# A two-layer hybrid decoder trunk in float32: tables loaded in pieces, adaptation sums and small DVE jobs moved, attention transposes and the key's rotary sum reordered

## What is computed

```python
for l in range(DEPTH):
    mod = c_act @ ada_w[l] + ada_b[l]                       # 6 * 1024 numbers from one vector c
    h = modulate(rmsnorm(x, mix_pre_g[l]), sh_m, sc_m)
    t = h @ w_in                                            # 1024 x 6816
    y_lru = rglru_branch(...) @ lru_wo                      # conv, gates, softplus(-lambda), linear scan
    y_ret = retention_branch(...) @ ret_wo                  # rotary q and k, decayed scores, group norm
    y_mla = mla_branch(...) @ mla_wo                        # low-rank q and kv, 8 heads, causal softmax
    merged = gates[0] * y_lru + gates[1] * y_ret + gates[2] * y_mla
    x = x + g_m * rmsnorm(merged @ w_out, mix_post_g[l])
    x = x + g_f * rmsnorm(conv_glu(h2, w_up, conv, w_down), ffn_post_g[l])
```

## Time and profile before

| | us |
|---|---|
| median of 3 runs | 958.68 (957.09 to 959.09) |
| the profiled execution, own time | 959.5 |
| its span in the trace | 957.7 |
| PE busy | 931.6 (97%) |
| DVE busy | 731.3 (76%) |
| ACT busy | 522.7 (55%) |
| DMA | 206.36 MB, mean 215 GB/s |

### The profile page before, as it was taken

One profiled execution on the slowest core, in us unless ns is written; L12 is line 12 of the kernel. 1 busy time (PEld: TensorE's weight loads), 2 busy tenths in 40 slices (PEclk: granted clock), 3 DMA queues, 4 the chain that ended last, 5 costly groups with the idle time before them and its releaser, 6 DMA issues.

```text
span 957.7 us, 17447 instructions
## 1 busy us (share of the span) xinstructions
PE 931.6 (97%) x6840; PEld 863.5 (90%) x6840; DVE 731.3 (76%) x988; ACT 522.7 (55%) x693; POOL 43.7 (5%) x85
## 2 busy tenths in 40 slices
PE   6999999999999999999999999999999999999997
PEld 6889899889987999999979999989999799999996
DVE  4969968877787878887786877887768776676666
ACT  4445756445557655454673475743446675554553
POOL 0000000100000000000000000000000000000000
PEclk9999999999999999999999999999999999999999
DMA  9995757775583676766645775767666455655451
GB/s 351 327 287 194 230 200 262 239 240 200 186 295 113 231 254 245 256 241 199 203 170 169 252 240 189 248 210 236 207 230 233 163 176 179 216 175 179 146 202 44
DMA packets 134427, 206.36 MB, mean 215 GB/s; under 512 B 6497, under 2 KB 104801, under 8 KB 134241
## 3 DMA queue, kind: packets, MB, share of 16 engines
q1 hardware_dynamic: 122704, 162.08, 51.5%
q0 software_dynamic: 11520, 41.95, 12.0%
q10 hardware_dynamic: 144, 1.51, 0.5%
HBM read 204.47 MB, written 1.05 MB: 215 GB/s over the span
## 4 chain that ended last, share of the span: by engine, by line
PE 80%; DVE 11%; DMA 3%; ACT 2%; issue 2%; SPq 1%; DVEq 0%; ACTq 0%; POOLq 0%
PE banks L1705 73%; DVE w_lo L1097 3%; DVE adw L1090 2%; DMA h<-in_ada_rows 1%; DMA raw<-in_w_in 1%; DMA adw<-in_ada_rows 1%; SPq L463 1%; PE banks L1995 1%; PE banks L1985 1%; PE banks L1988 1%; ACT h_hi L656 1%; PE banks L1816 1%; DVE EF L1607 1%; PE banks L1862 0%; PE banks L2004 0%
## 5 line engine op out<-in xcount | busy, mean ns | idle before, releaser
L1705 PE MATMUL banks<-h_lo,w_hi 128*128 128x256 f32 x1504 | 426.0, 283 | 5.9 <-DVE h_lo L1158 2.2
L1705 PE MATMUL banks<-h_hi,w_lo 128*128 128x256 f32 x1504 | 420.7, 280 | 0.0
L1705 PE MATMUL banks<-h_hi,w_hi 128*128 128x256 f32 x1504 | 420.4, 280 | 0.0
L1705 PEld LDWEIGHTS banks<-h_lo,w_hi 128*128 128x128 f32 x1504 | 283.3, 188 | 10.9 <-issue 4.9
L1705 PEld LDWEIGHTS banks<-h_hi,w_lo 128*128 128x128 f32 x1504 | 283.5, 188 | 2.3 <-issue 1.4
L1705 PEld LDWEIGHTS banks<-h_hi,w_hi 128*128 128x128 f32 x1504 | 283.4, 188 | 0.0
L1097 DVE TENSOR_TENSOR w_lo<-raw,w_hi 128x2048 fp32r<-128x2048 f32 x96 | 219.4, 2289 | 47.0 <-ACT w_hi L598 46.5
L598 ACT ACTIVATE w_hi<-raw 128x2048 fp32r<-128x2048 f32 x96 | 182.7, 1912 | 103.6 <-PE banks L1705 82.0
L1607 DVE SCALAR_TENSOR_TENSOR EF<-banks,par,EF 128x254 f32<-128x254 f32 (+1 forms) x176 | 76.8, 478 | 57.6 <-ACT EF L949 51.8
L1631 DVE TENSOR_TENSOR w_lo<-raw,w_hi 128x2048 fp32r<-128x2048 f32 x42 | 96.0, 2286 | 21.1 <-ACT w_hi L968 21.1
L968 ACT ACTIVATE w_hi<-raw 128x2048 fp32r<-128x2048 f32 x42 | 80.4, 1913 | 36.7 <-PE banks L1705 36.7
(11 more groups left out here) (275 smaller groups left out, 1210.8 us busy)
## 6 DMA issues: line engine op xcount, KB each, us to landing
raw<-in_w_in SPq DMA_DIRECT2D x52, 1024.0 KB, 5.8
raw<-in_ffn_w_up SPq DMA_DIRECT2D x44, 1024.0 KB, 5.1
adw<-in_ada_rows POOLq DMA_DIRECT2D x80, 512.0 KB, 4.9
raw<-in_ffn_w_down SPq DMA_DIRECT2D x22, 1024.0 KB, 4.9
raw<-in_w_out SPq DMA_DIRECT2D x8, 1024.0 KB, 7.3
raw<-in_ret_wo SPq DMA_DIRECT2D x4, 1024.0 KB, 6.7
raw<-in_lru_wo SPq DMA_DIRECT2D x4, 1024.0 KB, 6.9
raw<-in_mla_wo SPq DMA_DIRECT2D x4, 1024.0 KB, 7.1
```

What stands on the lines that cost most here:

```text
L1705: ins = MM(ps, lhs, rhs, start=first and n == 0, stop=last and n == 2)
```

## The change

The table comes in six pieces, issued by SP behind blocks 4 to 9: the rotation matrices first, then the decays two heads at a time, then the mask. PE's first rotation waits for the first piece only, and DVE waits for the rest ahead of the key's rotary sum of layer 0. The LRU gate weights are loaded by POOL, those of layer 0 when block 2 has its high part, those of layer 1 behind tile 25. The first two tiles wait for block 7 instead of 3. The adaptation sums of blocks 7 to 12 are gone; `merge_sums` has one more in m = 4 and 6 and two more in m = 8 and 9. The second `angles` and the stages of `softplus` stand earlier in DVE's and ACT's lists. The key's rotary sum stands ahead of the first two `ret_scores`. Both `head_scales` stand behind both value products. For even m below 8, the transposes stand behind the branch product, and `mla_av` stands in the middle of the next gate product; ACT's copy stands behind the split. The loop of POOL is the same loop in two parts.

```diff
--- before.py
+++ after.py
@@ -288,6 +288,8 @@
 
         col = {**COL, "-8sp": P + 120, "8sp": P + 124}
 
+        TABLES = [(NFIRST, c0), *((c0 + 2 * i * T, c0 + 2 * (i + 1) * T) for i in range(HEADS // 2)), (c0 + HEADS * T, NCONST)]
+
         def PC(l, name, i=0, n=1):
             return par[:, l, col[name] + i:col[name] + i + n]
 
@@ -300,7 +302,7 @@
         ADA0 = 2 * DK
 
         c_in, cst_in, pos_in, x_in, vec_in = (sem(n) for n in ("c_in", "cst_in", "pos_in", "x_in", "vec_in"))
-        tables_in = sem("tables_in")
+        rotations_in, tables_in = sem("rotations_in"), sem("tables_in")
         ada_in = [sem(f"ada_in{i}") for i in range(ADA0 // 2 + 1)]
         cbc_ps, cbc_ev = sem("cbc_ps"), sem("cbc_ev")
         ada0_used, ada0_red, wbd_zero = sem("ada0_used"), sem("ada0_red"), sem("wbd_zero")
@@ -482,13 +484,9 @@
                         sp.dma_start(pos_i, A["positions"][0, :].partition_broadcast(P)).then_inc(pos_in, 16)
                         sp.dma_start(par[:, 0, 0:2 * P], A["vectors"][:, 0, 0:2 * P]).then_inc(vec_in, 16)
                         sp.dma_start(par[:, 1, :], A["vectors"][:, 1, :]).then_inc(vec_in, 16)
-                    if j == 4:
-
-                        sp.wait_ge(wbd_zero, 1)
-                        for m, name in enumerate(("lru_wa", "lru_wx")):
-                            for b in range(2):
-                                blockw = A[name][bass.ds(l, 1)].rearrange("a (i b) h k -> (a b) h i k", b=2)[b]
-                                sp.dma_start(wbd[64 * b:64 * b + 64, m, :, 64 * b:64 * b + 64], blockw).then_inc(wbd_in.s, 16)
+                    if l == 0 and 4 <= j < 4 + len(TABLES):
+                        a, b = TABLES[j - 4]
+                        sp.dma_start(cst[:, a:b], consts[:, a:b]).then_inc(rotations_in if j == 4 else tables_in, 16)
 
                 def up(l, c0, n):
                     return A["ffn_w_up"][bass.ds(l, 1)].rearrange("a (k p) n -> p (a k) n", p=P)[:, :, bass.ds(c0, n)]
@@ -536,21 +534,38 @@
 
             ada_v = A["ada_rows"].rearrange("l (t p) d -> p (l t) d", p=P)
             TILES = 2 * NT * L - ADA0
-            assert TILES % 2 == 0
+            assert TILES % 2 == 0 and L == 2
 
             def load(n, slot):
                 pool.dma_start(adw[:, slot, :], ada_v[:, bass.ds(n + ADA0, 1), :].rearrange("p a d -> p (a d)")).then_inc(adw_in[slot], 16)
 
             pool.wait_ge(ada0_red, ADA0 - len(ON_PE))
             pool.wait_ge(ada0_used, len(ON_PE))
-            pool.wait_ge(hi_ready.s, hi_ready.at(0, 4))
+            def recurrence_weights(l):
+
+                for m, name in enumerate(("lru_wa", "lru_wx")):
+                    for b in range(2):
+                        blockw = A[name][l].rearrange("(i b) h k -> b h i k", b=2)[b]
+                        pool.dma_start(wbd[64 * b:64 * b + 64, m, :, 64 * b:64 * b + 64], blockw).then_inc(wbd_in.s, 16)
+
+            def next_tiles(first, last):
+
+                with pool.Fori(first // 2, last // 2) as it:
+                    for slot in range(2):
+                        pool.wait_ge(ada_red.s, it * 2 + (1 + slot))
+                        pool.sem_inc(tick, 1)
+                        load(it * 2 + (2 + slot), slot)
+
+            pool.wait_ge(wbd_zero, 1)
+            pool.wait_ge(hi_ready.s, hi_ready.at(0, 3))
+            recurrence_weights(0)
+            pool.wait_ge(hi_ready.s, hi_ready.at(0, 8))
             load(0, 0)
             load(1, 1)
-            with pool.Fori(0, TILES // 2 - 1) as it:
-                for slot in range(2):
-                    pool.wait_ge(ada_red.s, it * 2 + (1 + slot))
-                    pool.sem_inc(tick, 1)
-                    load(it * 2 + (2 + slot), slot)
+            next_tiles(0, NT)
+            pool.wait_ge(lr_ev.s, lr_ev.at(0, 2))
+            recurrence_weights(1)
+            next_tiles(NT, TILES - 2)
 
 
 
@@ -739,12 +754,15 @@
 
                 split_block(l, 3)
                 if l == 0:
-                    act.dma_start(cst[:, NFIRST:NCONST], consts[:, NFIRST:NCONST]).then_inc(tables_in, 16)
                     act.wait_ge(vec_in, 48)
                 for j in range(4, 9):
                     split_block(l, j)
-                    if l == 0 and j in (4, 8):
-                        sines((0, 2)[j // 8])
+                    if l == 0 and j in (4, 6):
+                        sines(j - 4 if j == 4 else 2)
+                    if l == 0 and j == 7:
+                        softplus_exp()
+                    if l == 0 and j == 8:
+                        softplus_log()
 
                 for i in range(2):
                     product_done(act, l, J[("lx", i)])
@@ -753,8 +771,6 @@
                                scale=PC(l, "lru_conv_w", 12 + t), bias=PC(l, "lru_conv_b", t))
                     a.then_inc(lx_c0.s, 1)
                     split_block(l, 9 + i)
-                    if l == 0:
-                        (softplus_exp, softplus_log)[i]()
 
 
                 def lru_gates(i):
@@ -912,9 +928,11 @@
                     if m == 9:
                         attended_high(1)
                     gate(m)
-                    if m % 2 == 0 and 2 <= m <= HEADS:
+                    if m == HEADS:
                         transposed(m // 2 - 1)
                     split_block(l, j + RING + m % 2)
+                    if m in (2, 4, 6):
+                        transposed(m // 2 - 1)
                     if m == 6:
                         attended_high(0)
                     if m % 2 == 1 and m < HEADS:
@@ -1283,8 +1301,8 @@
                 V.scalar_tensor_tensor(flat2(CD, c).rearrange("p (h n) -> p h n", n=64), vsum[:, c, :].unsqueeze(2).to_broadcast([P, 8, 64]),
                                        -1.0 / 64, heads, ALU.mult, ALU.add).then_inc(v_ev.s, 1)
 
-            mixer_sums = {j: n for n, j in enumerate(range(7, 21))}
-            merge_sums = (2, 1, 2, 1, 2, 1, 2, 1, 1, 1, 2, 2)
+            mixer_sums = {j: n for n, j in enumerate(range(13, 21))}
+            merge_sums = (2, 1, 2, 1, 3, 1, 3, 1, 3, 3, 2, 2)
             assert len(mixer_sums) + sum(merge_sums) == NT + DK
 
             def mixer_split(l, j):
@@ -1322,16 +1340,18 @@
                 dve.wait_ge(trig_ready, 2)
                 rope_parts(0)
                 mixer_split(l, 5)
+                if l == 0:
+                    angles(sinm, cosm, inv_mla)
+                    softplus(0)
                 rope_parts(1)
                 mixer_split(l, 6)
                 mixer_split(l, 7)
+                if l == 0:
+                    softplus(1)
                 rope_parts(2)
                 rope_sum(0)
                 rope_parts(3)
                 rope_sum(1)
-                if l == 0:
-                    angles(sinm, cosm, inv_mla)
-                    softplus(0)
                 mixer_split(l, 8)
 
                 def ret_scores(h):
@@ -1374,12 +1394,10 @@
                 rope_sum(2)
                 mixer_split(l, 9)
                 if l == 0:
-                    softplus(1)
+                    softplus(2)
                 rope_sum(3)
                 lru_taps(1)
                 mixer_split(l, 10)
-                if l == 0:
-                    softplus(2)
                 latent_low(0)
                 latent_low(1)
                 mixer_split(l, 11)
@@ -1410,9 +1428,11 @@
 
                 dve.wait_ge(lr_ev.s, lr_ev.at(l, 2))
                 V.tensor_tensor(h32[:, 0:4, :], h32[:, 0:4, :], EF[:, 0:4, :], ALU.mult).then_inc(l_ix.s, 1)
+                if l == 0:
+                    dve.wait_ge(tables_in, 16 * (len(TABLES) - 1))
+                rotary_key_sum()
                 ret_scores(0)
                 ret_scores(1)
-                rotary_key_sum()
                 silu(0)
                 mixer_split(l, 14)
                 dve.wait_ge(cs_sd.s, cs_sd.at(l, 1))
@@ -1809,7 +1829,7 @@
 
                 def rotate(i):
                     if i == 0:
-                        pe.wait_ge(tables_in, 16)
+                        pe.wait_ge(rotations_in, 16)
                         pe.wait_ge(v_ev.s, v_ev.at(l, 4))
                     pe.wait_ge(rot_c.s, rot_c.at(l, i + 1))
                     pe.wait_ge(rot_t.s, rot_t.at(l, i + 1))
@@ -1974,7 +1994,8 @@
                         ins = mm3(PS[:, (2, 6)[c], :], (wh[:, k, 1, :], wl[:, k, 1, :]),
                                   (ob_hi[:, QK + k, cs], ob_lo[:, QK + k, cs]), k == 0, k == KVK - 1, weights_move=True)
                     ins.then_inc(uv_ps.s if c == 0 else blk_used.s, 1)
-                    head_scales(c)
+                head_scales(0)
+                head_scales(1)
 
                 def mla_scores(p):
                     if p >= 1:
@@ -2059,11 +2080,15 @@
                 mla_scores(0)
                 merge_product(1)
                 for m in range(2, HEADS):
-                    merge_gate(m)
+                    if m > 2 and m % 2 == 1:
+                        merge_gate(m, (0,))
+                        mla_av(m // 2 - 1)
```

(6 more changed lines are left out.)

## The result

| | before | after |
|---|---|---|
| median, us | 958.88 (957.09 to 959.22, 4 runs) | 989.67 (987.92 to 991.93, 4 runs) |
| profiled execution, own time | 959.5 | 989.04 |
| span | 957.7 | 987.3 |

The ratio is 1.0326 (95% interval 1.0301 to 1.0352): 30.8 us slower, 3.7 us above the forecast of 986 and inside its range. In the kernel after the change the lines of PE stand 20 lower than before, those of DVE 18 to 20 lower: the product is L1725, the transposes L2016, the sum L1108, the split L1115, the probabilities L1546.

The account below looks back on a forecast made before the run. PE was taken as the bound, busy 931.6 of 957.7 us; 959.5 - 8.2 + 35.6 = 986.9 us for the profiled execution, so a median of 986 us, range 979 to 996 (chance 0.62).

Parts of the forecast that it names:

- Part 4: Merge stage: a third sum in a row must wait for its tile, so PE waits; +35.6 us for two layers.
- 2.24 + L1 + L2: PE's wait for block 34, L1 and L2 being two tile trips of m = 8 and 9; 10.5 us a layer.
- m = 4 and 6: Merge-stage threes: m = 4 costs 0, up to 2.4 us; m = 6 makes PE wait 4.1 us before transposes.
- The clock: PE runs at the lower clock behind its waits of 4.1 and 10.5 us; 3.2 us a layer, 0 if it holds.
- Part 1: Table in pieces, weights and first tiles on POOL: PE's wait for block 4's split goes; -1.5 us.
- Part 2: Mixer: PE's waits for the key go in both layers, with layer 0's time at the lower clock; -3.8 us.
- Part 3: Transposes behind the branch product: PE's waits for the scaled probabilities go, about 0.1 us a layer staying; -2.9 us.
- The sum of gains: Gains of tables, key and transposes together, 1.5 + 3.8 + 2.9 = 8.2 us.
- (a): Rival: waits come but mild, trips of 3.7 us everywhere and the clock holds; 972 us, up to 978; chance 0.18.
- (c): Rival: the third tile is there in time in the merge stage, only the gains remain; 950 us; chance 0.06.
- (b): Rival: heavy, 7.0 us trips where tiles crowd, m = 4 waits, block 4 stays slow; 996 to 1004 us; chance 0.12.
- The four weight loads between tiles 25 and 26: POOL in layer 0 has 5 us for them before tile 26: cost nothing, or up to 3 us.

Follow-up runs that it names:

- e1: The changed kernel with the adaptation sums back where they were before and POOL's first two tiles at block 4's high part; 951.47 us, ratio 0.9926.
- e2: The kernel before with only the adaptation sums moved as in the change; 996.57 us, ratio 1.0397.
- e3: The changed kernel with the splits of blocks 34 and 35 ahead of the three sums of m = 9; 981.75 us, ratio 1.0238.
- e8: The changed kernel with two sums in every m of the merge stage, never three in a row; 969.05 us, ratio 1.0115.
- e4: The changed kernel with one sum each in m = 8 and 9 and four sums back behind blocks 9 to 12; 965.53 us, ratio 1.0083.
- e6: The changed kernel with 22 dummy products on PE behind the gate product of m = 10; 986.9 us, ratio 1.0299.
- e10: e1 with the whole table loaded by ACT in one DMA at block 3 again; 952.57 us, ratio 0.9929.
- e9: e1 with the key's rotary sum behind the first two ret_scores again; 952.3 us, ratio 0.993.
- e7: e1 with the transposes of m = 2, 4, 6 ahead of the branch product again and mla_av behind it; 954.4 us, ratio 0.9967.

## Why the prediction was right, point by point

**Part 4 is the loss, by its own chain.** The price of 35.6 us was 38.2 by e1 and 38.1 by e2. For m = 8 and 9 the formula 2.24 + L1 + L2 gives 2.24 + 5.2 + 3.7 = 11.1 with the trips of after against 10.94 measured, and in layer 1, where both trips took 3.8, 9.8 against 9.57. The prediction had 10.5 for both, with 4.45 and 3.8. e3 shows that the split behind the sums carries the wait to PE, e8 that the order of the sums makes DVE's waiting.

The wait is not DVE's idle time alone. In layer 0 DVE stood 4.83 + 2.06 + 1.24 = 8.1 us for tiles. The four sums more are 4 x 1.15 = 4.6 us of work, from start to start. Against this 1.1 us went into the idle time ahead of merge(9), and block 34 used to be split 0.7 us before PE wanted it (260.35 + 2.25 against 263.27): 8.1 + 4.6 - 1.1 - 0.7 = 10.9. The same sum gives 3.5 + 2.3 - 1.8 = 4.0 for e8, where 4.00 was measured. So about 2.8 us a layer would stay, an estimate, even if every tile came in time. And the prediction's sentence that two sums in a row always find their tiles is wrong where two steps follow closely: in e8 they did not.

The Trainium skill (DMA: Bandwidth & Descriptors, "Anatomy of one DMA") gives 3.2 us for such a tile by its fit, an estimate, and so a wait of 8.6. The shortest trip of the stage took 3.6 us, 0.4 above it, and those on DVE's path 3.7 to 6.9, so the rows decided rightly.

**m = 4 and 6.** m = 4 was put at 0, up to 2.4. That was the wrong end: 0.96 and 1.91 us, because the tile took 5.5 us in layer 0 and 6.6 in layer 1, not the median of 4.6. m = 6 was put at 4.1; after shows 3.39 and 2.15, since PE came to the transposes later by m = 4's wait. The two are not additive. Without the threes behind, e4 has 4.07 and 3.34. Together both places and their clock cost 7.0 us a layer by e4 (7.5 by the ratios); the prediction had 4.1 and half of the clock, 5.7.

**The clock.** 3.2 us a layer were predicted; the trace has 2.7 + 1.5 = 4.2 in layer 0 and 1.5 + 2.1 = 3.6 in layer 1 (the same products from start to end, after minus before). e6 confirms it by taking it away for the wait at m = 10: 3.5 us in two layers by the traces, 2.8 by the medians, against 3.6. It was wrong in one detail: I expected it behind the transposes' wait in both layers. In layer 1 the wait was 2.15 us and the clock held; instead it fell behind the 1.91 us of m = 4. Which of these waits brings the fall varies between executions: in e6, which differs from after only at m = 10, it fell behind the transposes' waits of 3.61 and 3.68 us in both layers and behind neither of m = 4.
The Trainium skill (TensorE: Matmul & The Clock Gate, "HAM oscillation") has idle gaps paid twice, and the runs agree for the long ones: with e6's products in the gap the second payment is gone.

**Part 1**, -1.5: block 4's trip is 6.3 us instead of 10.57, and the wait of 1.48 us is gone; PE stands 2.0 us earlier at the first rotation, 0.44 of them from a wait for the first half of x that varies between executions (0.36 to 2.6 us). e10 has 1.27 us of it back in the trace. The reason held too: with the table away ACT no longer waits for the block, but for PE to free the slot.

**Part 2**, -3.8: layer 0 gained 3.1 (5.1 less 2.0) against 3.2, but layer 1 only 0.3 against 0.57, as 0.20 us of waiting for `lat_rc` came in its place. The named cause was enough, but not the only one. The prediction put the wait down to the six sums and the four decay products ahead of the key's sum. e2 takes away the six sums alone, and the wait of layer 0 falls from 1.62 to 0.57 us, without the slow product behind it. e1 has all six sums back and no such wait; e9 has the decays ahead again as well, and its wait is 0.64 us, again without the slow product. So the decays are worth the last 0.6 us, and the other 1.0 with the 1.60 of clock goes by either of two things: by taking the six sums away (e2), or by something that e9 still has of the change, the earlier `angles` and `softplus`, the table in pieces, or the later first tiles. Which of these was not tried alone.

**Part 3**, -2.9: e7 gives 2.9 to 3.9, and its trace has the 3.1 us of waits back.

**The sum of gains**, 8.2: 7.0 between medians, 5.5 to 8.6 by the interval. Taken back one by one 2.9 + 0.8 + 1.1 = 4.8 between medians; the other 2.2, near what can be told, belong to no part that was tried alone. They are about the 1.0 + 1.60 us of the key in layer 0 that e9 does not bring back.

**Rivals.** (a), mild trips and a full clock, fell by the trip of 5.2 us and the stretches at 0.50 to 0.60. (c), the tile in time, fell with DVE's 38.8 us of waiting; its 950 us was also too low for its own condition, by the 2.8 us a layer above. (b), heavy, was right on m = 4, and near with one trip of 6.9 us at m = 6 of layer 1. The four weight loads between tiles 25 and 26 cost nothing, as predicted: POOL was done with them at 262.27 and still stood 3.01 us for DVE.

**The better kernel** is e1: keep the gains, leave the sums. A third slot for the tiles was not tried, because the loops of the feed-forward half count them in pairs.

## What to carry to other kernels

A list of work with idle time in it can't take more work by that alone: with n buffers (two here), at most n consumers may stand closer together than one load's trip, and each one more costs up to a whole trip, here 3.7 to 6.9 us for an instruction of 1.2. The work itself is paid as well once it stands ahead of something that is wanted at once. Put what another engine waits for (here the splits) ahead of an instruction that may itself wait. And when one edit of four loses, undo that one alone: the rest was worth 7 us.

## What was not expected of the hardware

A float32 product of 128x256 outputs whose operands aren't in the rounded form took two instructions of 0.215 us, 0.43 in all, against 0.117 for one pass of the rounded form. And the length of a gap alone doesn't say whether the clock falls: it did behind 1.62 us before, 1.91 us after and 2.17 in e2, and not behind 1.48 before, 2.15 after and 2.69 in e2. Even the same gap ahead of the same product went both ways. PE waits for the low part of the first half of x until 39 us, 2.36 us in e1 and 2.35 in e9, which are the same program up to there; these are the stretches behind it, e1's first:

```profile
40.00:43.20 3.20, 3.20 (x15) 2.57 (x14) 2.72 (x3) 2.34 (x2) 2.12 (x4) 1.00 0.10 33
40.00:43.20 3.20, 3.20 (x9) 2.43 (x8) 2.92 (x4) 2.08 (x2) 2.36 (x4) 0.50 0.16 46
```

What tells the two cases apart no run here shows. So a single trace can differ from another of the same kernel by such a fall, about 1.7 us, and a difference of that size should be read from several executions.
